# Two more column groups of a decoder layer's projections as seven quarter products

## The chip, the cores and the metric

The kernel runs on one core of a Trainium2 chip. TensorE (PE) multiplies, VectorE (DVE) and ScalarE (ACT) prepare operands and empty the accumulators, GpSimd (POOL) moves rows of tokens, and SyncE (SP) issues the loads. The metric is the device time of one execution in microseconds; lower is better.

## The reference

One decoder layer for 576 tokens (512 of a prompt, 64 of samples) with 1024 channels in float32. Cut to what the change touches:

```
z = h @ w_in                      # 1024 x 6400 columns
q, k, v, c_b, c_c, c_h, g_a, g_c = split(z)
attn = windowed attention of q, k, v
conv = c_b * short_conv(c_c * c_h)          # three taps along the tokens
merged = sigmoid(g_a) * (attn @ w_attn_out) + sigmoid(g_c) * (conv @ w_conv_out)
h = layer_norm(a * h + merged @ w_o)
h = layer_norm(a * h + experts(h) + shared(h) + ple(h))   # 64 routed experts, 6 per token
```

## The kernel before

**Groups.** The weights of the projections are loaded 256 columns at a time. Such a column group gives 2 x 128 output channels for all 576 tokens. float32 precision comes from a split of both operands into a high and a low part: a product is hi*hi + hi*lo + lo*hi. `split_hi` on ACT writes the high part of a group's weights, `split_lo` on DVE the low part (one instruction of 128x2048 each). `Step(base).v` is the number of a group; even and odd groups use one of two weight buffers each (`w_raw`, `w_hi`, `w_lo`).

**A full group** (`group`, L1225 through `chunk`) is 2 halves of channels x 8 chunks of the contraction x 3 terms x 2 halves of tokens = 96 matmuls of 288 columns, into the four banks of `proj`.

**A group in seven products** (`seven_products`, L1414 through `quarter_product`) uses Strassen's scheme in Winograd's form: weights (A) and tokens (B) are cut into 2 x 2 quarters, and 7 quarter products of 4 chunks x 3 terms = 12 matmuls each, 84 in all, give the four corners of the result. They go into the four banks of `att`, in the order a11*b11 (bank 0), s1*t1 (bank 2), s2*t2 (bank 1), s3*t3 (bank 3), a12*b21 (bank 0), s4*b22 (bank 2), a22*t4 (bank 3). A product that comes back to a bank waits until its earlier contents have been read. DVE forms the weights' sums (`s3_sum`, `s1_sum`, `s2_sum`, `s4_sum`), ACT their high parts (`s3_high`, `s12_high`, `s4_high`, `block_hi` for the plain quarters) and DVE the low ones (`block_lo`, `s3_low`, `s12_low`, `s4_low`). The sums of the tokens (t1 to t4: `t_difference`, `t_less`, `t_low`) are made once, while the attention output groups run. Results come back through `first_copy` (ACT, bank 0), `first_sums` (banks 1 and 2), `next_sums` (bank 3) and three `corner` additions (DVE).

**Order of the groups on TensorE**: attention inputs, the first two groups of the convolution, four attention output groups (`G_AO`, numbers 11 to 14), convolution groups n = 2 to 11 (numbers 15 to 24), and then four times a gate group and a convolution output group (`G_GC` = 25 and on; here GC0, CO0, GC1, CO1 ...). A triple of the convolution is n = 3m, 3m+1, 3m+2: the channels c_c, c_h and c_b. `conv_taps(m)` multiplies c_c and c_h and forms the three taps, `conv_gated(m)` multiplies by c_b and splits the result into `mix_hi` and `mix_lo`, which the CO groups read. `SEVEN` lists the n that run as seven products; the gates GC1 to GC3 do too. The order of each engine is written out by hand, an engine takes its instructions in that order, and semaphores hold them back. The waits that matter: the first product of a seven-product group waits for the low parts of its blocks (`w_ready`) and for the first corner of the seven-product group before it (`dve_read(s - 1, 3)`); the sixth waits for `first_sums` of its own group (`dve_read(s, 1)`), the seventh for `next_sums`. A CO group waits for the gate's sigmoid (`mm_free`). SP issues a load when the group two before has been split, and behind a seven-product group only when its sixth product is done, since `w_rest` lies in the raw weights.

Behind the groups come the output projection, norm, routing, shared expert and the routed experts, whose weights (192 MB) are loaded into a ring of three buffers.

## Time and profile before

| | us |
|---|---|
| median of 3 runs | 1236.82 (1236.31 to 1236.92) |
| the profiled execution | 1233.74 |
| its span, first to last instruction | 1231.9 |
| PE busy | 1195.2 (97% of the span) |
| DVE busy | 587.8 (48%) |
| ACT busy | 354.2 (29%) |
| chain that ended last | PE 50%, DMA 42%, DVE 4% |

The profile comes from one execution. Times in its rows are microseconds from the first instruction. A busy PE has matmuls in flight; since they are pipelined, the time of a group is read from its start to the next one's. Idle time in square brackets is that of the engine just before the row, with what ended it. An instruction of DVE or ACT that follows another without a wait starts some 0.1 us before that one's end, so the distance of two starts is what one costs in a row of them.

### The profile page before, as it was taken

What the parts mean: (1) busy time and instruction counts of PE and PEld (TensorE: products, weight loads), DVE (VectorE), ACT (ScalarE), POOL (GpSimd) and SP (SyncE); (2) the same over time, 40 slices, a digit from 0 to 9 for tenths busy, and PEclk for the clock granted to TensorE, in tenths of its full rate; (3) what the DMA queues carried; (4) which work ended last, traced back from release to release, by engine and by line L of the source; (5) the groups of instructions that cost most, each with busy time, mean ns of one, the idle gap of its engine ahead of it and who ended that gap; (6) DMA issues with size and microseconds to landing.
All of it is one profiled execution on the core that took longest, in us unless ns stands there. A gap on an engine that the chain in (4) does not pass through costs nothing.

```text
span 1231.9 us, 23531 instructions
## 1 busy us (share of the span) xinstructions
PE 1195.2 (97%) x8676; PEld 941.2 (76%) x8677; DVE 587.8 (48%) x1292; ACT 354.2 (29%) x704; POOL 141.5 (11%) x211
## 2 busy tenths in 40 slices
PE   8999999999999999999999999999999999999877
PEld 8999979999999999989998665555565555655543
DVE  4667774556887666677882112112212222112138
ACT  4365562333434342325022111111111111111121
POOL 0300000000000000003133121112111112121100
PEclk9999999999999999999999999999999999999999
DMA  8222123221333143624539999999999999999996
GB/s 270 75 69 69 45 64 76 42 92 44 103 103 104 38 135 93 211 82 153 229 143 367 418 420 418 421 420 421 419 420 420 420 420 418 420 422 421 422 370 282
DMA packets 98663, 307.40 MB, mean 250 GB/s; under 512 B 11244, under 2 KB 62404, under 8 KB 72840
## 3 DMA queue, kind: packets, MB, share of 16 engines
q1 hardware_dynamic: 85332, 275.20, 57.7%
q0 software_dynamic: 12304, 28.60, 6.0%
q10 hardware_dynamic: 948, 2.50, 0.6%
q8 instruction: 56, 0.92, 0.3%
q14 instruction: 23, 0.19, 0.0%
HBM read 294.45 MB, written 26.94 MB: 261 GB/s over the span
## 4 chain that ended last, share of the span: by engine, by line
PE 50%; DMA 42%; DVE 4%; issue 1%; DVEq 1%; POOL 0%; ACT 0%; SPq 0%; ACTq 0%; POOLq 0%
DMA w_exp<-in_w_e_down_dram 40%; PE proj L1225 23%; PE att L1414 8%; PE proj L1484 4%; PE proj L1635 3%; PE att L1357 1%; PE att L1319 1%; DMA fold<-expert_rows 1%; PE att L1493 1%; PE proj L1259 1%; PE proj L1579 1%; PE att L1579 1%; PE att L1370 1%; DVE res L2609 1%; PE att L1484 1%
## 5 line engine op out<-in xcount | busy, mean ns | idle before, releaser
L1709 PE MATMUL att<-w_exp,xt 128*64 128x256 f32 x2560 | 286.3, 380 | 9.1 <-DMA w_exp<-in_w_e_up_dram 7.0
L1709 PEld LDWEIGHTS att<-w_exp,xt 128*64 128x64 f32 x2560 | 191.3, 137 | 113.7 <-issue 36.2
L1729 PE MATMUL proj<-w_exp,ht_e 128*64 128x512 f32 x640 | 146.2, 598 | 3.9 <-DMA w_exp<-in_w_e_down_dram 3.9
L1225 PE MATMUL proj<-h_hi,w_hi 128*128 128x288 f32 x480 | 106.2, 303 | 0.3 <-DVE w_lo L523 0.3
L1225 PE MATMUL proj<-h_lo,w_hi 128*128 128x288 f32 x480 | 102.2, 294 | 0.0
L1225 PE MATMUL proj<-h_hi,w_lo 128*128 128x288 f32 x480 | 102.2, 295 | 0.0
L1729 PEld LDWEIGHTS proj<-w_exp,ht_e 128*64 128x64 f32 x640 | 44.2, 136 | 75.9 <-issue 71.6
L2556 DVE TENSOR_SCALAR ysb<-proj,tabw 128x512 f32 x40 | 30.0, 751 | 132.0 <-PE proj L1729 132.0
L1225 PEld LDWEIGHTS proj<-h_hi,w_hi 128*128 128x128 f32 x480 | 75.9, 189 | 6.1 <-issue 4.6
L1225 PEld LDWEIGHTS proj<-h_lo,w_hi 128*128 128x128 f32 x480 | 77.2, 188 | 0.0
L1225 PEld LDWEIGHTS proj<-h_hi,w_lo 128*128 128x128 f32 x480 | 77.0, 188 | 0.0
L2551 DVE TENSOR_TENSOR h_e<-sg,att 128x128 f32<-128x128 f32 x80 | 19.5, 286 | 116.5 <-PE att L1709 116.5
L2546 DVE TENSOR_TENSOR sg<-sg,att 128x256 f32<-128x256 f32 x40 | 16.9, 422 | 119.1 <-ACT sg L1177 119.1
L523 DVE TENSOR_TENSOR w_lo<-w_raw,w_hi 128x2048 fp32r<-128x2048 f32 x24 | 55.0, 2290 | 27.1 <-ACT w_hi L513 23.2
L1180 ACT ACTIVATE ht_e<-att 128x128 f32<-128x128 f32 x80 | 18.9, 278 | 167.9 <-PE att L1715 167.9
L1185 ACT ACTIVATE ysb<-proj,tabw 128x512 f32 x40 | 27.5, 688 | 133.2 <-PE proj L1729 133.2
L513 ACT ACTIVATE w_hi<-w_raw 128x2048 fp32r<-128x2048 f32 x24 | 45.8, 1910 | 50.5 <-PE proj L1225 37.3
L1645 PEld LDWEIGHTS proj<-ident,xg 128*128 128x128 f32 x328 | 43.6, 196 | 17.1 <-issue 12.7
L1645 PE MATMUL proj<-ident,xg 128*128 128x128 f32 x328 | 53.9, 287 | 1.5 <-DMA xg<-x_rows,gidx_col 1.5
L1225 PE MATMUL proj<-mix_hi,w_hi 128*128 128x288 f32 x256 | 54.6, 295 | 0.0
L1225 PE MATMUL proj<-mix_hi,w_lo 128*128 128x288 f32 x256 | 54.6, 295 | 0.0
L1225 PE MATMUL proj<-mix_lo,w_hi 128*128 128x288 f32 x256 | 54.5, 295 | 0.0
(475 smaller groups left out, 2292.4 us busy)
## 6 DMA issues: line engine op xcount, KB each, us to landing
w_exp<-in_w_e_gate_dram SPq DMA_DIRECT2D x64, 1024.0 KB
w_exp<-in_w_e_up_dram SPq DMA_DIRECT2D x64, 1024.0 KB
w_exp<-in_w_e_down_dram SPq DMA_DIRECT2D x64, 1024.0 KB
w_raw<-in_w_in_dram SPq DMA_DIRECT2D x21, 1024.0 KB
part<-expert_rows SPq DMA_DIRECT2D x8, 1536.0 KB, 21.3
w_raw<-in_w_in_dram SPq DMA_DIRECT2D x8, 512.0 KB
w_raw<-in_w_attn_out_dram SPq DMA_DIRECT2D x8, 512.0 KB
w_raw<-in_w_conv_out_dram SPq DMA_DIRECT2D x4, 1024.0 KB
```

The source lines that it names most:

```text
L513: nc.scalar.activation(w_hi[:, g.par, :], w_raw[:, g.par, :], ACT.Copy).then_inc(hi_done, 1)
L523: nc.vector.tensor_tensor(w_lo[:, g.par, :], w_raw[:, g.par, :], w_hi[:, g.par, :].bitcast(F32), ALU.subtract).then_inc(w_ready, 1)
L1185: nc.scalar.activation(ysb[:, bass.ds(side_of, 1), 0:512].rearrange("p o n -> p (o n)"), proj[:, 2, :], ACT.Copy, scale=tabw[:, bass.ds(k, ...
L1225: last = nc.tensor.matmul(proj[:, 2 * i + a, 0:HALF], lhs, x[:, c, a * HALF:(a + 1) * HALF], start=(c == 0 and n == 0), stop=(c == KC - 1 ...
L1414: last = nc.tensor.matmul(att[:, bank, 0:HALF], left[a][:, c, :], right[b][:, c, :], start=(c == 0 and n == 0), stop=(c == Q - 1 and n == 2))
L1484: last = nc.tensor.matmul(out, x, v, start=(c == 0 and n == 0), stop=(c == KC - 1 and n == last_term))
L1579: last = nc.tensor.matmul((proj, att)[m][:, 2 * k + a, 0:HALF], v[:, c, m * P:(m + 1) * P], x[:, c, a * HALF:(a + 1) * HALF], start=(c == ...
L1635: last = nc.tensor.matmul(gate_bank(u), x[:, c, t * P:(t + 1) * P], v[:, c, :], start=(c == 0 and n == 0), stop=(c == KC - 1 and n == 2))
L1645: last = nc.tensor.transpose(proj[:, half, c * P:(c + 1) * P], xg[:, :, half * 4 + c], ident[:, :])
L1709: last = nc.tensor.matmul(att[e * SLOT:(e + 1) * SLOT, m, 0:FF], xt[:, c, e * SLOT:(e + 1) * SLOT], weights[e][:, c, :], start=(c == 0), s ...
L1729: last = nc.tensor.matmul(proj[e * SLOT:(e + 1) * SLOT, 2 + half, :], ht_e[:, c, e * SLOT:(e + 1) * SLOT], down[e][:, c, half * 512:(half ...
L2556: nc.vector.tensor_scalar(ysb[:, bass.ds(side_of, 1), 512:D].rearrange("p o n -> p (o n)"), proj[:, 3, :], tabw[:, bass.ds(k, 1)], None, A ...
```

## The change

Two more groups run as seven quarter products: n = 2, the last group of the first convolution triple (`SEVEN` begins with 2), and the gate group GC0. Their sums and splits have places of their own in the orders of DVE and ACT, and the loads behind them wait for their sixth product.

```diff
-SEVEN = (4, 5, 7, 8, 10, 11)
+SEVEN = (2, 4, 5, 7, 8, 10, 11)
...
             for it in range(1, 4):
-                if it > 1:
-                    sp.wait_ge(st_mm, product_done(len(SEVEN) + it - 2, 5))
+                sp.wait_ge(st_mm, product_done(len(SEVEN) + it - 1, 5))
                 load(Step(G_GC + 2 * it), w_in, COL_GC + it * GW)
...
@@ ACT, while the attention output groups run
+                if k < 3:
+                    split_hi(act, Step(G_AO + k + 1))
+                else:
+                    for i in range(4):
+                        act.wait_ge(sum_raw, N_STEP + i + 1)
+                        nc.scalar.activation(t_hi[i][:, :, :], t_raw[i][:, :, :], ACT.Copy).then_inc(sum_hi, 1)
+                    block_hi(Step(G_CONV[2]))
+                    s3_high(Step(G_CONV[2]), 0)
+                    s12_high(0)
+                    s4_high(Step(G_CONV[2]), 0)
...
@@ ACT, convolution groups n = 2, 5, 8, 11
-                    first_tap(m)
+                    if m:
+                        first_tap(m)
                     first_copy(n, s)
-                    new_state(m)
-                    split_hi(act, g)
+                    if m:
+                        new_state(m)
+                    if n < 11:
+                        split_hi(act, g)
+                    else:
+                        block_hi(g)
+                        s12_high(s + 1)
+                        s4_high(g, s + 1)
+                        s3_high(g, s + 1)
+                        act.wait_ge(st_mm, product_done(s + 1, 1))
+                        act.wait_ge(u_done, 2 * m + 3)
+                        nc.scalar.activation(sig_c[:, 0, 0:HALF], att[:, 0, 0:HALF], ACT.Copy).then_inc(st_act, 1)
+                        split_hi(act, Step(G_GC + 1))
...
@@ PE
             for it in range(4):
-                if it:
-                    seven_products(Step(G_GC + 2 * it), len(SEVEN) + it - 1, moved=True)
-                else:
-                    group(Step(G_GC), h_hi, h_lo)
+                seven_products(Step(G_GC + 2 * it), len(SEVEN) + it, gate=it)
+                if it == 0:
                     pe.wait_ge(cv_lo, KC)
                 group(Step(G_GC + 2 * it + 1), mix_hi, mix_lo)
...
@@ DVE, convolution groups n = 2, 5, 8, 11
+                    if n == 2:
+                        first_sums(s)
                     next_sums(s)
-                    split_lo(dve, g)
-                    corner_11(G_CONV[n])
-                    corner_12(s)
-                    corner_21(G_CONV[n])
+                    if n < 11:
+                        split_lo(dve, g)
+                        corner_11(G_CONV[n])
+                        corner_12(s)
+                        corner_21(G_CONV[n])
+                    else:
+                        block_lo(g)
+                        s1_sum(g, s + 1)
+                        s2_sum(g, s + 1)
+                        s4_sum(g)
+                        corner_11(G_CONV[n])
+                        corner_12(s)
+                        s12_low(s + 1)
+                        corner_21(G_CONV[n])
+                        s3_sum(g, s + 1)
+                        s3_low(g, s + 1)
+                        s4_low(g, s + 1)
                     conv_gated(m)
```

For GC0 the order in which the weights' sums are made and counted is s1, s2, s4, s3 and not s3, s1, s2, s4, and `seven_products` waits for them by these counts.

**VectorE, while the attention output group number 14 runs.** Before, from the split of group 15 (n = 2) to the split of group 16:

```order
L523 TENSOR_TENSOR w_lo<-w_raw,w_hi 128x2048 [waits hi_done]
L2060 TENSOR_TENSOR gate_a<-proj,gate_a 128x576 [waits mm_ready0,sga]
L2060 TENSOR_TENSOR gate_a<-proj,gate_a 128x576 [waits mm_ready1]
L2050 TENSOR_TENSOR t_lo_98<-t_raw_102,t_hi_94 128x1152 [waits e_ready]
L2050 TENSOR_TENSOR t_lo_99<-t_raw_103,t_hi_95 128x1152 [waits e_ready]
L2050 TENSOR_TENSOR t_lo_100<-t_raw_104,t_hi_96 128x1152 [waits e_ready]
L2050 TENSOR_TENSOR t_lo_101<-t_raw_105,t_hi_97 128x1152 [waits e_ready]
L523 TENSOR_TENSOR w_lo<-w_raw,w_hi 128x2048 [waits hi_done]
```

Of the changed kernel, from the last of the t sums' low parts on:

```order
L2064 TENSOR_TENSOR t_lo_101<-t_raw_105,t_hi_97 128x1152 [waits e_ready]
L2072 TENSOR_TENSOR w_diff<-w_raw 128x4x128 [waits mm_ready1,w_dma1]
L2081 TENSOR_TENSOR s_raw<-w_raw 128x512 [waits st_out]
L2089 TENSOR_TENSOR s_raw<-s_raw,w_raw 128x512
L2102 TENSOR_TENSOR w_lo<-w_raw,w_hi 128x4x128 [waits hi_done]
L2102 TENSOR_TENSOR w_lo<-w_raw,w_hi 128x4x128 x2
L2095 TENSOR_TENSOR w_raw<-w_raw,s_raw 128x4x128
L2109 TENSOR_TENSOR w_lo<-w_diff,w_hi 128x4x128 [waits e_ready]
L2116 TENSOR_TENSOR s_lo<-s_raw,s_hi 128x512 [waits e_ready] x2
L2122 TENSOR_TENSOR w_rest<-w_raw,s_hi 128x4x128 [waits e_ready]
L2143 TENSOR_TENSOR gate_a<-proj,gate_a 128x576 [waits mm_ready0,sga]
L2143 TENSOR_TENSOR gate_a<-proj,gate_a 128x576 [waits mm_ready1]
```

The low parts of the t sums moved ahead of the last two gate products, and one split has become the preparation of a seven-product group.

**VectorE, from the next sums of n = 11 on**, that is behind the third tap of the last triple. Before (`w_lo` of the first row is GC0's, of the last CO0's; the three L2147 are the corners of n = 11):

```order
L523 TENSOR_TENSOR w_lo<-w_raw,w_hi 128x2048 [waits hi_done]
L2147 TENSOR_TENSOR prod_90<-att,prod_90 128x288 [waits mm_ready0]
L2147 TENSOR_TENSOR prod_90<-att,prod_90 128x288 [waits lg_ready]
L2147 TENSOR_TENSOR prod_91<-att,prod_91 128x288 [waits mm_ready1]
L2011 TENSOR_TENSOR prod_90<-prod_90,y_cv_88 128x512
L2012 TENSOR_TENSOR prod_90<-prod_90,y_cv_88 128x64
L2011 TENSOR_TENSOR prod_91<-prod_91,y_cv_89 128x512
L2012 TENSOR_TENSOR prod_91<-prod_91,y_cv_89 128x64
L2024 TENSOR_TENSOR mix_lo<-prod_90,mix_hi 128x576 [waits cv_hi]
L2024 TENSOR_TENSOR mix_lo<-prod_91,mix_hi 128x576 [waits cv_hi]
L523 TENSOR_TENSOR w_lo<-w_raw,w_hi 128x2048 [waits hi_done]
```

In the changed kernel the same place begins with these (the corners are L2170):

```order
L2102 TENSOR_TENSOR w_lo<-w_raw,w_hi 128x4x128 [waits hi_done]
L2102 TENSOR_TENSOR w_lo<-w_raw,w_hi 128x4x128 x2
L2081 TENSOR_TENSOR s_raw<-w_raw 128x512 [waits lg_ready]
L2089 TENSOR_TENSOR s_raw<-s_raw,w_raw 128x512 [waits lg_ready]
L2095 TENSOR_TENSOR w_raw<-w_raw,s_raw 128x4x128
L2170 TENSOR_TENSOR prod_90<-att,prod_90 128x288 [waits mm_ready0]
L2170 TENSOR_TENSOR prod_90<-att,prod_90 128x288 [waits lg_ready]
L2116 TENSOR_TENSOR s_lo<-s_raw,s_hi 128x512 [waits e_ready] x2
L2170 TENSOR_TENSOR prod_91<-att,prod_91 128x288 [waits mm_ready1]
L2072 TENSOR_TENSOR w_diff<-w_raw 128x4x128 [waits mm_ready1,w_dma1]
L2109 TENSOR_TENSOR w_lo<-w_diff,w_hi 128x4x128 [waits e_ready]
L2122 TENSOR_TENSOR w_rest<-w_raw,s_hi 128x4x128 [waits e_ready]
```

Behind them stand the four instructions of `conv_gated`, and then:

```order
L2038 TENSOR_TENSOR mix_lo<-prod_90,mix_hi 128x576 [waits cv_hi]
L2038 TENSOR_TENSOR mix_lo<-prod_91,mix_hi 128x576 [waits cv_hi]
L523 TENSOR_TENSOR w_lo<-w_raw,w_hi 128x2048 [waits hi_done]
L2156 TENSOR_TENSOR u_120<-att,sig_c 128x288 [waits lg_ready,pt_read]
L2158 TENSOR_TENSOR sig_c<-att,u_120 128x288
L2164 TENSOR_TENSOR sig_c<-att,sig_c 128x288 [waits lg_ready]
```

The one split of GC0 has become nine instructions around the corners, and the results of GC0 (from L2156 on) are read behind the split of CO0.

**ScalarE, behind the high parts of the last mix.** Before:

```order
L1036 ACTIVATE t_moved_hi<-t_hi_94 128x1152
L1036 ACTIVATE t_moved_lo<-t_lo_98 128x1152
L513 ACTIVATE w_hi<-w_raw 128x2048 [waits mm_ready1,w_dma0]
L1051 ACTIVATE sig_c<-proj 128x576 [waits mg_ready,mm_ready0]
L1051 ACTIVATE sig_c<-proj 128x576 [waits mg_ready,mm_ready1]
L1054 ACTIVATE h_hi<-t_hi_95 128x4x288
L1054 ACTIVATE h_lo<-t_lo_99 128x4x288
L950 ACTIVATE w_hi<-w_raw 128x4x128 [waits mm_ready1,w_dma1]
```

Changed:

```order
L1062 ACTIVATE sig_c<-sig_c 128x576 [waits lg_read] x2
L1065 ACTIVATE t_moved_hi<-t_hi_94 128x1152
L1065 ACTIVATE t_moved_lo<-t_lo_98 128x1152
L1067 ACTIVATE h_hi<-t_hi_95 128x4x288
L1067 ACTIVATE h_lo<-t_lo_99 128x4x288
L942 ACTIVATE w_hi<-w_raw 128x4x128 [waits mm_ready1,w_dma1]
```

All four copies of t1 and t2 now stand behind GC0's second sigmoid and before the blocks of GC1.

## Rows read from the trace of the kernel before

**Rows 1.** The chain of waits in order of time: start, us, what.
```profile
217.45 84.20 PE proj L1225 x630
...
371.73 22.25 PE att L1414 x168
393.98 25.58 PE proj L1225 x192
419.57 11.13 PE att L1414 x84
...
667.38 10.65 DMA w_exp<-in_w_e_down_dram
```

**Rows 2.** Two stretches: us, busy us of PE, PEld, DVE, ACT, POOL, clock, DMA.
```profile
393.98:406.77 12.79, 12.79 (x99) 12.79 (x98) 5.88 (x9) 5.83 (x6) 0.00 (x0) 1.00 0.66 215
490.70:667.00 176.30, 174.12 (x1317) 165.62 (x1317) 123.25 (x307) 49.30 (x73) 36.33 (x32) 1.00 0.50 183
```

**Rows 3.** Time line of DVE during attention output group 14: start, us, instruction.
```profile
263.96 1.35 DVE L2033 TENSOR_TENSOR t_raw<-h_hi 128x1152 f32<-128x1152 f32 x1
...
269.54 1.36 DVE L2043 TENSOR_TENSOR t_raw<-t_raw,h_lo 128x1152 f32<-128x1152 f32 x1
...
276.76 5.16 DVE L2050 TENSOR_TENSOR t_lo<-t_raw,t_hi 128x1152 fp32r<-128x1152 f32 x4
```

**Rows 4.** Time line of DVE, the preparation of n=4.
```profile
291.25 0.69 DVE L2076 TENSOR_TENSOR w_diff<-w_raw 128x512 f32<-128x512 f32 x1
291.85 0.69 DVE L2085 TENSOR_TENSOR s_raw<-w_raw 128x512 f32<-128x512 f32 x1
292.63 0.69 DVE L2093 TENSOR_TENSOR s_raw<-s_raw,w_raw 128x512 f32<-128x512 f32 x1
293.24 1.89 DVE L2106 TENSOR_TENSOR w_lo<-w_raw,w_hi 128x512 fp32r<-128x512 f32 x3
295.23 0.69 DVE L2099 TENSOR_TENSOR w_raw<-w_raw,s_raw 128x512 f32<-128x512 f32 x1
...
296.44 1.29 DVE L2120 TENSOR_TENSOR s_lo<-s_raw,s_hi 128x512 fp32r<-128x512 f32 x2
297.65 0.68 DVE L2126 TENSOR_TENSOR w_rest<-w_raw,s_hi 128x512 fp32r<-128x512 f32 x1
```

**Rows 5.** Time lines of SP and ACT: GC2's load is issued and first read.
```profile
429.13 0.39 SPq L549 DMA_DIRECT2D w_raw<-in_w_in_dram  x1
...
434.81 0.63 ACT L950 ACTIVATE w_hi<-w_raw 128x512 fp32r<-128x512 f32 x1 [2.90 <-DMA w_raw<-in_w_in_dram]
```

**Rows 6.** Time line of DVE at the end of n=11.
```profile
387.73 0.46 DVE L2133 TENSOR_TENSOR u<-att,prod 128x288 f32<-128x288 f32 x1 [0.61 <-PE att L1414]
...
391.09 2.28 DVE L523 TENSOR_TENSOR w_lo<-w_raw,w_hi 128x2048 fp32r<-128x2048 f32 x1
393.29 1.19 DVE L2147 TENSOR_TENSOR prod<-att,prod 128x288 f32<-128x288 f32 x3
394.57 0.69 DVE L2011 TENSOR_TENSOR prod<-prod,y_cv 128x512 f32<-128x512 f32 x1
...
396.46 1.43 DVE L2024 TENSOR_TENSOR mix_lo<-prod,mix_hi 128x576 fp32r<-128x576 f32 x2
```

**Rows 7.** Time line of ACT: a copy of t2, and GC1's second sigmoid.
```profile
408.41 1.16 ACT L1054 ACTIVATE h_lo<-t_lo 128x1152 fp32r<-128x1152 f32 x1
...
431.23 0.69 ACT L1047 ACTIVATE sig_c<-sig_c 128x576 f32<-128x576 f32 x1 [0.91 <-DVE sig_c L2147]
```

**Rows 8.** Time line of DVE: the second product of CO0's results.
```profile
419.68 0.76 DVE L2235 TENSOR_TENSOR prod<-proj,sig_c 128x576 f32<-128x576 f32 x1 [1.90 <-PE proj L1225]
```

**Rows 9.** Time line of PE at the start; waits of PE, 217 to 667 us.
```profile
1.07 5.38 PE L1238 MATMUL att<-warm 128*128 128x128 f32 x26 [1.07 <-POOL warm L740]
...
11.28 1.73 PE L1266 MATMUL proj<-warm 128*128 128x128 f32 x14
...
PE proj L1608 <- DVE tab_b L2475: 2.1, 2, 1.2
```

More of the change, by code:

```diff
@@ L973, in s4_high @@
                 nc.scalar.activation(s4_hi[:, :, :], quarter(w_raw, g, 1, 0), ACT.Copy).then_inc(sum_hi, 1)
+            for k in range(4):
+                nc.scalar.activation(gate_a[:, 2 * k:2 * k + 2, :], gate_a[:, 2 * k:2 * k + 2, :], ACT.Sigmoid).then_inc(sga, 1)
+                if k < 3:
[8 more added lines that the diff above has]
+                    s4_high(Step(G_CONV[2]), 0)
             def first_tap(m):
@@ L1416, in quarter_product, with seven_products @@
                 return last
-            def seven_products(g, s, moved=False):
+            def seven_products(g, s, gate=None):
                 a11, a12, s3, a22 = (tuple(quarter(w, g, k, n) for w in (w_hi, w_lo))
@@ L1425, in seven_products @@
                 t1, t2, t3, t4 = (tuple(v[k][:, :, :] for v in (t_hi, t_lo)) for k in range(4))
-                if moved:
+                if gate:
                     t1 = tuple(v[:, :, :] for v in t1_moved)
@@ L1429, in seven_products @@
                 s4 = (s4_hi[:, :, :], quarter(w_rest, g, 1, 0))
-                for i in range(0 if moved else 2):
+                for i in range(2 if gate is None else 0):
                     nc.tensor.sem_inc(mm_free[i], 1)
@@ L2110, in s3_low @@
             def s3_low(g, s):
[L2112 removed]
+                dve.wait_ge(sum_hi, sum_count(s, 4 if s == len(SEVEN) else 1))
                 nc.vector.tensor_tensor(quarter(w_lo, g, 0, 1), quarter(w_diff, g, 0, 1),
```

102 lines of the change are left out of this document (51 added, 51 removed).

## The prediction, written before the changed kernel ran

> **What bounds the kernel now.** I read the chain of waits first: from 217.45 us on it is TensorE alone, group after group without a gap (84.20 us of full groups, then 22.25 us for two seven-product groups, 25.58 us for two full ones, 11.13 us for one), up to the routing, and from 667.38 us on it is the loads of the expert weights [rows 1]. The table of stretches says the same: TensorE is busy for all 12.79 us of the first gate group at granted clock 1.00, and for 174.12 of the 176.30 us from there to the experts [rows 2]. The expert loads are issued when work on TensorE and VectorE is done, so what moves the end of the last gate group moves the end of the program by as much. Nothing behind it has a start of its own. The stretch to look at is therefore 217 to 491 us, and the question is only whether TensorE stays without gaps. The time lines of VectorE and ScalarE answer it.
>
> **What the change removes from TensorE.** A full group is 96 matmuls, a group in seven products 84. They cost 25.58 / 2 = 12.79 us and 11.13 us [rows 1], so each converted group saves 1.66 us, and two save 3.32 us if no product waits.
>
> **Group n=2 (the last of the first triple).** Its weights must now be prepared by VectorE while the last attention-output group runs (263.31 to 276.1 us). The last five instructions of the raw t sums (263.96 to 270.90, 6.9 us) come one group, 12.8 us, earlier and end at about 258; ScalarE has the four high parts at about 259.4. The four low parts (5.16 us, at 276.76 before) now stand where the raw sums stood, at 263.96 [rows 3], and end at about 269.1. The preparation of a seven-product group is the row of nine instructions that n=4 has at 291.25 to 298.33, 7.1 us [rows 4]. Put at 269.05 it gives the low parts of the blocks (all that the first product needs) at about 273.0, s1 and s2 by 275.5, s4 by 276.1. TensorE wants the first at 276.1 and s1 at 277.7. VectorE's two gate products of that group follow, at 276.05 and 276.7; nobody writes their banks before 287. The next group's load now waits for n=2's s4 product (285.6) and by the 5.7 us that such a load takes [rows 5] it lands at 291.3, and VectorE gets to it at about 291.1 anyway; its preparation ends at 298.5, its blocks at 295.2, against a start at 300.0. So n=2 has cover everywhere: **-1.66 us**.
>
> **The first gate group (GC0).** Here three seven-product groups follow each other (n=10, n=11, GC0), and VectorE's order is what counts. I use the profile's clock as if n=2 had not been made shorter. VectorE waits for TensorE for the last time at 387.73; from there it is busy without a break. At 391.09 it stood before the 2.20 us split of the full group, followed at 393.29 by the three corners (0.37 us apart) that free the att banks [rows 6]. Now it has, from 391.09: three block parts 1.81, s1 0.79, s2 0.78, s4 0.61 [rows 4]. The first corner starts at 395.08 and is done at 395.53. GC0's first product writes bank 0, which that corner reads, so it waits for it; n=11 ends at 393.98. That is a gap of 395.57 - 393.98 = **1.6 us**. Before, GC0 was a full group and wrote proj, so the corners did not hold it.
>
> From there on VectorE runs: two corners 0.74, s1 and s2 low 1.21, third corner 0.37, the s3 difference 0.69, ScalarE's high part of it 0.66 (which nothing fills), s3 low 0.60, s4 low 0.78 with the drain. The gated product begins at 400.2 instead of 394.57. It and the two low parts of mix take until 403.4 (394.57 to 397.81 before), the split of CO0's weights 2.20 more, to 405.6 [rows 6]. Only then comes the first sum of GC0 (two instructions of 0.46 us with a drain between them, 1.0 us): done at 406.6. TensorE has started GC0 at 395.57 and wants to begin its sixth product, which overwrites bank 2, after five of 1.59 us, at 403.5. The sixth waits for that first sum, so a second gap: 406.64 - 403.52 = **3.1 us**. The fifth to seventh product see no other wait: ScalarE's copy of bank 0 is done at about 399.1, the next sums by 407.5 against the seventh product at 408.2. GC0 ends at 409.8, where it ended at 406.77: 11.13 + 1.6 + 3.1 = 15.8 us against 12.79, **+3.0 us**. Put together: between the fourth product of n=11 and the sixth of GC0 VectorE has 16 us of work where TensorE has 12.7 (eight products of 1.59).
>
> Both bounds of this term: if ScalarE's 0.66 and all drains (0.1 each, four of them) could be hidden, it would be about 1.1 less; if CO0's load, which is issued at 392.4, lands as late as ScalarE could have noticed before (399.1), or the hand-overs cost 0.1 instead of 0.04, some 0.5 more. I take the middle, since the rows of n=4 and n=11 repeat to within 0.02 us.
>
> **The second gate (GC1) and later.** CO0 now starts at E = 409.8. GC1's load, which was issued at 393.40 before, waits for GC0's s4 product and lands near E + 4.1, as GC2's did (wait until 434.81 with the end of GC1 at 430.70) [rows 5]. ScalarE, though, first has the second sigmoid (it starts 0.53 after E, as at 431.23) and now all four copies of t1 and t2 (1.06 us each), two of which stood before the first gate until now. It gets to GC1's blocks at E + 5.4, and VectorE ends the preparation at E + 12.0 [rows 4, 7]. The two products of CO0's results come behind it, the second at E + 13.5 instead of E + 12.9 (419.68 against 406.77) [rows 8]. The chain to GC1's first sum then ends 8.1 us after GC1's start, not 7.5, and the sixth product wants it at 7.95: a gap of about **0.2 us**. GC2 and GC3 keep the pattern that they have.
>
> **The sum.** -1.66 + 3.0 + 0.2 = +1.6 us. The profiled execution took 1233.74 us, 1231.9 of it its span; it would become 1235.3 and 1233.5. The median of the runs shown, 3.1 us higher, goes from 1236.82 to **1238.4 us**.
>
> A row and a page differ over the size of the saving. Twelve fewer matmuls are 12 x 0.133 = 1.6 us by the rows [rows 1]. The Trainium skill (TensorE: Matmul & The Clock Gate, Back-to-back issue gap) puts the gap between isolated matmuls at N / 2.4 + 2.5 ns, 122.5 ns for 288 columns; as an estimate from that page, 24 matmuls save 2.94 instead of 3.32 us and the sum would be some 0.4 us higher. I stay with the rows.
>
> **The rivals.** (1) *VectorE keeps up* and both gaps are absent: the whole 3.32 us comes out, 1233.5 us. It needs the 16 us between 389 and 406 to shrink to 12.7. For it speaks that the same instructions for n=10 leave no gap; against it, that n=10 has no gated product, no mix and no full split between its preparation and the next first sum. In between lies a case in which one of the gaps is half of what I count: 1235.5 to 1237. (2) *The gap costs the clock*, the slower side: the only waits of TensorE that the view of waits lists between 217 and 667 us are two of 2.1 us together, at granted clock 1.00 [rows 2, 9], and now it stands for 3.1 us in one piece. If the matmuls behind it run as the first ones of the program did (26 fillers in 5.38 us, where 14 later ones took 1.73, 0.124 each), the loss is 5.38 - 26 x 0.124 = 2.2 us once [rows 9]: 1240.6 us. It decides from the point where GC0's second gap is long enough. Against it: the profile gives granted clock 1.00 even for those first 5.38 us, and its only lower stretch lies behind the last matmul of the program.
> The Trainium skill (the same page, Why this matters for your kernels) says that a long enough idle between bursts of matmuls sends the array back to half rate. That is this rival; no row of this trace shows it in mid-program.
> (3) *A load becomes late*: n=4's and GC1's loads are the two that are held back. Each has over 1 us of cover (ScalarE is busy until E + 5.4, n=4's blocks are ready 4.8 us early), so it would cost under 1 us and stays inside the forecast's range. That the change leaves the kernel's order as it was is excluded: the rows of the two orders differ as shown.
>
> **How the numbers follow.** The forecast (1237.4 to 1239.4) gets 0.65, the case between 0.08, VectorE keeping up 0.10, the clock 0.17. A measurement of this kernel can tell some 0.2%, 2.5 us, from no change. Faster than 1234.3: rival 1 and a little of the case between, 0.12. Slower than 1239.3: rival 2 and 0.05 of the forecast's upper end, 0.22. Within: 0.66. The range that leaves out rival 1 and the upper half of rival 2 is 1235.2 to 1240.8.
>
> **What would show it.** In the changed trace: an att group of 84 matmuls in 11.1 us where n=2 is; two TensorE gaps in GC0, about 1.6 us before its first product behind a corner on VectorE and about 3.1 us before its sixth behind the first sum; CO0's start 1.4 us later than 406.77 on the trace's clock (-1.66 + 3.05); a gap of 0.2 us or none in GC1. I am wrong if TensorE has no gap in GC0, if the corners start before 394, if n=2 or n=4 waits for its weights, or if the stretch behind 491 us changes in length.

## The result and the profile after

| | before | changed |
|---|---|---|
| median, us | 1235.99 (1233.79 to 1238.57, 20 runs) | 1238.01 (1235.76 to 1239.78, 20 runs) |
| ratio of the times, 95% interval | 1 | 1.0020 (1.0014 to 1.0026) |
| profiled execution and its span, us | 1233.74, 1231.9 | 1239.67, 1237.7 |
| n=2 to the end of CO3, us | 214.70 | 219.05 |

The change costs 0.2%, about 2.5 us (1.7 to 3.2). A second set of runs of the changed kernel gave 1.0027 (1.0017 to 1.0038). It is slower than before, by little. The last line of the table is the stretch in which all of the change lies. The chain of waits of the changed kernel (start, duration, what; x counts matmuls) shows where it became longer:

```profile
277.55 11.13 PE att L1427 x84
...
371.54 19.45 PE att L1427 x147
390.99 1.80 DVE w_lo L2102 x3
...
406.53 4.96 PE att L1427 x24
...
432.52 3.41 PE att L1427 x24
```

Before, this chain was TensorE without a break [rows 1]. n=2 is now a group of 84 matmuls in 11.13 us. But the chain leaves TensorE at 390.99 and comes back only at 406.53, for the last two products of GC0. Those 24 matmuls take 4.96 us where the same two products of GC1 take 3.41 (the last row). The time line of TensorE has three rows with idle time between 394 and 434 us:

```profile
395.48 0.37 PE L1427 MATMUL att<-h_hi,w_hi 128*128 128x288 f32 x1 [1.69 <-DVE prod L2170]
406.53 0.37 PE L1427 MATMUL att<-h_hi,s_hi 128*128 128x288 f32 x1 [2.86 <-DVE sig_c L2158]
432.52 0.37 PE L1427 MATMUL att<-h_hi,s_hi 128*128 128x288 f32 x1 [0.32 <-DVE sig_c L2158]
```

The first is GC0's first product, behind the first corner of n=11; the second is its sixth, behind the first sum; the third is GC1's sixth. VectorE's time line says what it did meanwhile, and answers [rows 6]:

```profile
390.91 1.89 DVE L2102 TENSOR_TENSOR w_lo<-w_raw,w_hi 128x512 fp32r<-128x512 f32 x3
...
394.88 0.81 DVE L2170 TENSOR_TENSOR prod<-att,prod 128x288 f32<-128x288 f32 x2
...
398.57 0.69 DVE L2109 TENSOR_TENSOR w_lo<-w_diff,w_hi 128x512 fp32r<-128x512 f32 x1 [0.70 <-ACT w_hi L949]
...
399.95 0.69 DVE L2025 TENSOR_TENSOR prod<-prod,y_cv 128x512 f32<-128x512 f32 x1
...
403.19 2.28 DVE L523 TENSOR_TENSOR w_lo<-w_raw,w_hi 128x2048 fp32r<-128x2048 f32 x1
405.39 0.45 DVE L2156 TENSOR_TENSOR u<-att,sig_c 128x288 f32<-128x288 f32 x1
405.92 0.46 DVE L2158 TENSOR_TENSOR sig_c<-att,u 128x288 f32<-128x288 f32 x1
```

The corner starts at 394.88, the gated product at 399.95, the split for CO0 at 403.19, and only then the first sum, done at 406.4. The 0.70 us in brackets is ScalarE's high part of s3. What the prediction did not have in its sum stands in the table of stretches (the columns are busy shares of PE, PEld, DVE, ACT and POOL, then the granted clock, the share of the DMA engines and GB/s):

```profile
403.70:406.50 2.80, 0.00 (x0) 0.00 (x1) 2.62 (x4) 0.00 (x0) 0.00 (x0) 1.00 0.00 0
406.50:407.00 0.50, 0.47 (x4) 0.50 (x4) 0.50 (x2) 0.00 (x0) 0.00 (x0) 1.00 0.00 0
407.00:408.00 1.00, 1.00 (x9) 1.00 (x8) 0.67 (x2) 0.00 (x0) 0.00 (x0) 0.77 0.00 0
408.00:409.00 1.00, 1.00 (x6) 1.00 (x6) 0.05 (x1) 0.00 (x0) 0.00 (x0) 0.50 0.00 0
409.00:410.00 1.00, 1.00 (x6) 1.00 (x6) 0.41 (x1) 0.56 (x1) 0.00 (x0) 0.50 0.01 3
410.00:411.00 1.00, 1.00 (x6) 1.00 (x6) 0.00 (x0) 0.12 (x1) 0.00 (x0) 0.53 0.67 90
411.00:412.00 1.00, 1.00 (x10) 1.00 (x9) 0.46 (x1) 0.00 (x1) 0.00 (x0) 1.00 1.03 354
```

TensorE stood still for 2.86 us, started again at 406.53, and from about 407.5 to 411 the granted clock was 0.50 (1.2 GHz, the lower of its two levels). TensorE is full in these rows. The number behind x counts every matmul that is in flight at some time in the row, so it says less than the starts do: in the time line the matmuls start 0.24 us apart at clock 0.50, four in a microsecond, and 0.133 us apart, seven or eight, at 1.00. That costs 4.96 - 3.41 = 1.6 us.

### The profile page after: what moved, and what is told of

The parts are those of the page before. It is cut to its first block, busy times and chain, and to the rows that moved or that the text cites. A ratio compares the mean times of both kernels' runs of the same rounds, so it can differ in the third digit from the quotient of the medians.

```text
span 1237.7 us, 23555 instructions
## 1 busy us (share of the span) xinstructions
PE 1197.6 (97%) x8652; PEld 941.1 (76%) x8653; DVE 602.9 (49%) x1324; ACT 359.1 (29%) x718; POOL 140.8 (11%) x211
## 4 chain that ended last, share of the span: by engine, by line
PE 49%; DMA 41%; DVE 6%; issue 1%; DVEq 1%; ACT 1%; SPq 0%; ACTq 0%; POOLq 0%
DMA w_exp<-in_w_e_down_dram 39%; PE proj L1238 20%; PE att L1427 9%; PE proj L1498 4%; PE proj L1649 3%; PE att L1370 1%; PE att L1332 1%; PE att L1507 1%; PE proj L1272 1%; PE proj L1593 1%; DMA fold<-expert_rows 1%; PE att L1593 1%; PE att L1383 1%; PE att L1676 1%; DVE res L2646 1%
## 5 line engine op out<-in xcount | busy, mean ns | idle before, releaser
L1238 PE MATMUL proj<-h_hi,w_hi 128*128 128x288 f32 x416 | 92.5, 304 | 0.3 <-DVE w_lo L523 0.3
L1238 PE MATMUL proj<-h_lo,w_hi 128*128 128x288 f32 x416 | 88.9, 295 | 0.0
L1238 PE MATMUL proj<-h_hi,w_lo 128*128 128x288 f32 x416 | 88.8, 295 | 0.0
L1238 PEld LDWEIGHTS proj<-h_hi,w_hi 128*128 128x128 f32 x416 | 65.6, 188 | 6.1 <-issue 4.6
L1238 PEld LDWEIGHTS proj<-h_lo,w_hi 128*128 128x128 f32 x416 | 67.0, 189 | 0.0
L1238 PEld LDWEIGHTS proj<-h_hi,w_lo 128*128 128x128 f32 x416 | 66.9, 189 | 0.0
L523 DVE TENSOR_TENSOR w_lo<-w_raw,w_hi 128x2048 fp32r<-128x2048 f32 x22 | 50.4, 2289 | 26.4 <-ACT w_hi L513 20.7
L810 POOL DMA_INDIRECT expert_rows<-ysb,sidx_col x39 | 39.5, 1012 | 124.8 <-DVE ysb L2593 124.8
```

The costliest lines, as they stand in the source:

```text
L523: nc.vector.tensor_tensor(w_lo[:, g.par, :], w_raw[:, g.par, :], w_hi[:, g.par, :].bitcast(F32), ALU.subtract).then_inc(w_ready, 1)
L810: pool.indirect_dma_start(out=rows_d[:, :], out_offset=bass.IndirectOffsetOnAxis(ap=sidx_col[i][:, 0:1], axis=0), in_=ysb[:, i, :], in_off ...
L1238: last = nc.tensor.matmul(proj[:, 2 * i + a, 0:HALF], lhs, x[:, c, a * HALF:(a + 1) * HALF], start=(c == 0 and n == 0), stop=(c == KC - 1 ...
```

## The experiments

I compare the kernels in two ways: by the ratio of times to runs of the kernel before on the same chip, and by the length of the stretch from the start of n=2 to the end of CO3 in the one profiled execution of each, which leaves out what happens elsewhere. One correction belongs to the stretch: a CO group takes 12.80 or 12.49 us, and the same kernel has either, so I count every CO group as 12.80 (+0.31 us for each short one).

| kernel | stretch, us | CO groups at 12.49 | as if all 12.80 | to before | ratio of the times (95%) |
|---|---|---|---|---|---|
| before | 214.70 | 2 | 215.32 | | 1 |
| changed | 219.05 | 0 | 219.05 | +3.7 | 1.0020 (1.0014 to 1.0026) |
| after_again | 219.03 | 0 | 219.03 | +3.7 | 1.0027 (1.0017 to 1.0038) |
| n2_only | 213.02 | 2 | 213.64 | -1.7 | 0.9989 (0.9978 to 1.0000) |
| n2_again | 213.60 | 0 | 213.60 | -1.7 | 0.9997 (0.9988 to 1.0006) |
| gc0_only | 220.22 | 1 | 220.53 | +5.2 | 1.0048 (1.0033 to 1.0063) |
| dve_more | 222.30 | 0 | 222.30 | +7.0 | 1.0049 (1.0035 to 1.0063) |
| fill | 217.44 | 0 | 217.44 | +2.1 | 1.0020 (1.0008 to 1.0031) |
| fill_again | 217.43 | 0 | 217.43 | +2.1 | 1.0021 (1.0010 to 1.0032) |
| sums_first | 215.84 | 1 | 216.15 | +0.8 | 0.9999 (0.9989 to 1.0009) |
| late_mix | 216.64 | 1 | 216.95 | +1.6 | 1.0006 (0.9997 to 1.0015) |
| keep_up | 215.83 | 0 | 215.83 | +0.5 | 0.9996 (0.9987 to 1.0005) |
| early_copies | 212.26 | 3 | 213.19 | -2.1 | 0.9977 (0.9968 to 0.9986) |

My theory: n=2 has cover and saves its 1.66 us; all of the loss is at GC0, where VectorE has more to do before GC0's first sum than TensorE gives it time for, because work for CO0 stands ahead of it, and the stop that this makes draws the half clock. The rivals: the loss comes from n=2 having let TensorE run ahead; VectorE's total work decides, whatever its order; the half clock has nothing to do with the stop.

**Each half of the change alone.**

n2_only is the changed kernel with its second half undone:

```diff
-                seven_products(Step(G_GC + 2 * it), len(SEVEN) + it, gate=it)
+                if it:
+                    seven_products(Step(G_GC + 2 * it), len(SEVEN) + it - 1, gate=it)
+                else:
+                    group(Step(G_GC), h_hi, h_lo)
```

gc0_only has its first half undone:

```diff
-SEVEN = (2, 4, 5, 7, 8, 10, 11)
+SEVEN = (4, 5, 7, 8, 10, 11)
```

The orders of VectorE, ScalarE and SyncE go with them in both kernels.

> Only group n=2 runs as seven products; the first gate group (GC0) is a full group of 96 matmuls again, with the orders of VectorE and ScalarE that the kernel before has there. My theory (the two conversions add up, n=2 is worth -1.66 us and GC0 costs all the rest): no gap of TensorE between 217 and 490 us, GC0 in 12.8 us, the time 1.7 us below the kernel before. Rival (the loads or the preparation behind n=2 have moved and cost something further on, so that n=2 has no gain of its own): the same time as the kernel before, with 11.13 us for n=2 in the trace and the gain lost between there and the end of the gates.

> Only GC0 runs as seven products; n=2 is a full group again and its preparation stands where the kernel before has it. By the trace of the changed kernel GC0 takes 17.7 us instead of 12.8: my theory (the two gaps and the half clock behind them belong to GC0 alone) expects gaps of 1.7 and 2.9 us before its first and sixth product, about 3.4 us at half clock behind them, and a time 4.0 to 5.5 us above the kernel before. If the half clock was an accident of the one execution that was profiled: 3.2 to 3.6 us above. Rival (the gaps come from n=2, which lets TensorE run ahead of VectorE by 1.66 us more): the gaps shrink to 0 and 2 us, and the time is within 1 us of the kernel before.

The chain of n2_only has TensorE alone again, two full groups in one piece behind n=10 and n=11:

```profile
369.72 22.26 PE att L1423 x168
391.98 25.58 PE proj L1234 x192
```

Its stretch is 1.68 us shorter than before with the same number of short CO groups, against 1.66 expected. The times say -0.11% and, in a second set (expected: 0.9987), -0.03%; both intervals reach -0.12%, and the first touches no change. The saving is as large as predicted in the trace; in the times it is about half of that and at the edge of what can be measured.

> The kernel with only n=2 converted, once more, beside the one with all copies moved early, to tell which of the two is the faster. Expected from its trace: 1.6 us below the kernel before (ratio 0.9987), every group from n=2 to CO3 without a gap.

gc0_only has the same gaps as the changed kernel, 1.68 and 2.86 us, and is 0.48% slower than before, 5.9 us where 4.0 to 5.5 were expected. The rival (n=2 makes the gaps by letting TensorE run ahead) is excluded: without n=2 the gaps are as long. In the stretch the two halves add up: -1.70 + 5.21 = +3.5, and the changed kernel has +3.7. Its rows of stretches show more on the clock:

```profile
406.00:407.00 1.00, 0.00 (x0) 0.00 (x0) 1.00 (x2) 0.00 (x0) 0.00 (x0) 1.00 0.00 0
407.00:408.00 1.00, 0.00 (x0) 0.00 (x0) 0.83 (x3) 0.00 (x0) 0.00 (x0) 0.74 0.00 0
408.00:409.00 1.00, 0.94 (x4) 0.97 (x5) 0.99 (x3) 0.00 (x0) 0.00 (x0) 0.50 0.00 0
```

Here the clock falls while TensorE is still standing (PE busy 0.00 in the row with 0.74); in the changed kernel it fell when TensorE had been running again for about 1 us. So it isn't the restart that draws it.

**The half clock.** Two kernels test whether it belongs to the stop: one with the stop filled, one with a longer stop.

fill, in `seven_products` ahead of the sixth product:

```diff
                 pe.wait_ge(sum_ready, lo_count(s, 4))
+                if gate == 0:
+                    for _ in range(20):
+                        nc.tensor.matmul(proj[:, 0, 0:HALF], h_hi[:, 0, 0:P], h_hi[:, 0, 0:HALF], start=True, stop=True)
                 pe.wait_ge(st_dve, dve_read(s, 1))
```

dve_more, on VectorE in the loop over the gates:

```diff
+                if it == 0:
+                    dve.wait_ge(hi_done, G_GC + 2)
+                    nc.vector.tensor_tensor(w_lo[:, 0, :], w_raw[:, 0, :], w_hi[:, 0, :].bitcast(F32), ALU.subtract)
+                    dve.drain()
                 split_lo(dve, Step(G_GC + 2 * it + 1))
```

> The changed kernel with 20 extra matmuls of 288 columns (2.7 us at 0.133 each) between the fifth and the sixth product of GC0, where TensorE waits for VectorE's first sum. They write a bank that nothing reads before it is overwritten, and the results do not change. Theory A (the stop of 2.9 us is what halves the clock for the 3.4 us behind it): granted clock 1.00 through the whole of GC0, the sixth and seventh product in 3.2 us, the time 1.8 us below the changed kernel. Theory B (the lower clock comes from the whole pattern of the last 15 us, or is an accident of one execution): the time equals the changed kernel's, and the stretch at half clock is still there, or was not usual in it.

> The changed kernel with the split of CO0's weights done twice on VectorE (2.3 us more with its drain, the same values written), ahead of GC0's first sum. Theory (VectorE is what the sixth product waits for, one to one): the second gap grows from 2.9 to 5.1 us and CO0 starts 2.3 us later: 2.3 us above the changed kernel. The clock: if a longer stop of TensorE draws the half clock more surely, there is a stretch at half clock behind it in the trace, and the time is up to 1.8 us more than that, 2.3 to 4.1 us above. If the half clock has nothing to do with the stop, the time is 2.3 us above and the profiled execution has such a stretch in this place no more often than elsewhere.

> The changed kernel itself once more, beside the others on the same chip. The trace shows whether the half clock behind GC0's second gap, and the one at 175 us long before the change, are there in every execution. If they belong to the gap: again a stretch at half clock within 2 us of the end of the gap. If they are drawn anew in each execution: one of the two or both are missing, and the span is shorter by 1.7 us for each one missing ahead of 660 us. The time: 2 to 3 us above the kernel before.

> The kernel with 20 extra matmuls in GC0's second gap once more. Its trace showed no half clock behind the gap and 1.6 us less between n=2 and the end of CO3 than the changed kernel, while the medians of the two stood at the same ratio to the kernel before. If the half clock belongs to the gap: again none at 407 us, and the time 0.5 to 2 us below the changed kernel, whose two ratios were 1.0020 and 1.0027. If the gain of the trace is given back elsewhere: the ratio is again 1.002 or more.

The stretches at the end of the stop, of after_again, of fill_again and of dve_more:

```profile
407.00:408.00 1.00, 1.00 (x7) 1.00 (x6) 0.19 (x1) 0.00 (x0) 0.00 (x0) 0.55 0.00 0
408.00:409.00 1.00, 1.00 (x6) 1.00 (x6) 0.46 (x1) 0.08 (x1) 0.00 (x0) 0.50 0.00 0
```

```profile
408.00:409.00 1.00, 1.00 (x10) 1.00 (x9) 0.24 (x1) 0.69 (x1) 0.00 (x0) 1.00 0.20 29
```

```profile
407.00:408.00 1.00, 0.00 (x0) 0.00 (x0) 1.00 (x2) 0.00 (x0) 0.00 (x0) 0.61 0.00 0
408.00:409.00 1.00, 0.29 (x1) 0.32 (x2) 0.83 (x3) 0.00 (x0) 0.00 (x0) 0.50 0.00 0
...
413.00:414.00 1.00, 1.00 (x6) 1.00 (x6) 0.00 (x0) 0.14 (x1) 0.00 (x0) 0.50 0.57 115
414.00:415.00 1.00, 1.00 (x9) 1.00 (x8) 0.43 (x1) 0.00 (x0) 0.00 (x0) 0.97 0.97 327
```

after_again shows both answers to its question: the stretch at 175 us is missing and the one behind GC0's gap is there. All four profiled executions in which GC0 has a stop of 2.85 us or more (the changed kernel twice, gc0_only, dve_more) have the half clock there; both with the stop filled have 1.00 all through GC0, and their stretch is 1.6 us shorter for it. With a stop of 5.2 us, in one execution, the lower level lasts twice as long, about 6.8 us. dve_more's stretch is 3.25 us longer than the changed kernel's: 2.37 for the longer stop, which is one to one what was added on VectorE (2.3), and 0.9 because the last two products took 5.84 us instead of 4.96. By the ratios it is 2.7 to 3.6 us above the changed kernel (3.1 by the medians on the chip where both ran), inside the expectation with the clock. The half clock belongs to the stop, then, and theory A holds in the trace. The rule of the Trainium skill that the prediction named (TensorE: Matmul & The Clock Gate, Why this matters for your kernels) says that idle between bursts sends the array back to half rate. These four traces agree; but it speaks of longer stops than those of 1.65 to 2.6 us elsewhere in the program, behind which the clock fell in some of the executions here (below), and there the measurement decides.

The times don't confirm the 1.6 us. fill stands at 1.0020 and 1.0021, the changed kernel at 1.0020 and 1.0027: a difference of -0.1 to 0.9 us with an uncertainty of more than 1, between runs that did not stand side by side. From the end of CO3 to the end of the program, the two executions with the filled stop took 742.0 us each and the two of the changed kernel 741.1 and 740.6. The granted clock of that part says where this can come from. Both filled executions have three stretches of 3.4 us at 0.50 there (at 803, 1165 and 1192 us), the changed kernel has one (at 807) and after_again none, behind stops that the other kernels have there or close by. One such place, of after_again and of fill, each behind a stop of 2.6 us:

```profile
805.00:806.00 1.00, 1.00 (x12) 0.83 (x10) 0.00 (x0) 0.00 (x0) 0.00 (x0) 1.00 1.01 418
```

```profile
804.00:805.00 1.00, 1.00 (x8) 0.66 (x6) 0.00 (x0) 0.00 (x0) 0.00 (x0) 0.50 1.01 422
```

Over all 13 traces this part takes 741.6 to 743.1 us in the five with two or three such stretches, and 740.3 to 741.5 us in the eight with one or none. So the clock further on can give back as much as the filled stop gained. Whether filling the stop brings these stretches about or they fell there by chance is not shown (late_mix, which isn't filled, has the same three). What the half clock behind GC0's stop costs in the time is therefore between 0 and 1.6 us.

**The order on VectorE.**

sums_first moves the split for CO0, on VectorE in the loop over the gates:

```diff
-                split_lo(dve, Step(G_GC + 2 * it + 1))
+                if it:
+                    split_lo(dve, Step(G_GC + 2 * it + 1))
                 first_sums(s, raw_gate)
                 next_sums(s, raw_gate)
                 corner_11(G_GC + 2 * it, raw_gate)
+                if it == 0:
+                    split_lo(dve, Step(G_GC + 1))
```

> The changed kernel with one instruction moved on VectorE: the split of CO0's weights (2.2 us) stands behind GC0's first sums, next sums and first corner, no longer ahead of them. Theory (the sixth product waits for what VectorE is made to do first, so the order decides): first sum ready at 404.3 instead of 406.5, the gap before the sixth product 0.7 us instead of 2.9, no stretch at half clock; then CO0 waits for the split, the second corner and the sigmoid, about 2 us, and starts 2.8 us earlier than in the changed kernel: 1235.2 us. If the half clock is not usual in the changed kernel: 1.0 us below it. Rival (VectorE's total work up to CO0 decides, whatever its order): the gap only moves from the sixth product to the start of CO0, which starts where it did, and only the half clock, if it goes, changes the time.

One instruction in another place takes 0.21% off the changed kernel's 0.20%: the time is that of the kernel before. The list of waits of TensorE (waiting group, what it waited for: us in total, times, longest):

```profile
PE att L1427 <- DVE prod L2170: 1.7, 1, 1.7
PE proj L1238 <- ACT sig_c L1062: 1.2, 1, 1.2
PE att L1427 <- DVE sig_c L2158: 0.7, 1, 0.7
```

The gap before the sixth product is 0.7 us as expected, there is no stretch at half clock, and a new wait of 1.2 us stands before CO0, for the sigmoid. The sum of the gaps fell from 4.6 to 3.6 us and the half clock's 1.6 went with it: CO0 starts 131.5 us behind n=2 instead of 133.9, 2.4 us earlier where 2.8 were expected. Order decides more than the total does, but the wait at CO0 shows that the total was still too much. The next kernel takes away from that place what CO0 alone needs.

In late_mix TensorE's wait for mix moves from ahead of CO0 into `chunk`:

```diff
+                if c == KC - 2 and i == 0 and g.base == G_GC + 1 and g.v == G_GC + 1:
+                    pe.wait_ge(cv_lo, KC)
```

VectorE's `conv_gated(3)` no longer follows `s4_low` of n=11, and in the loop over the gates:

```diff
-                split_lo(dve, Step(G_GC + 2 * it + 1))
+                if it:
+                    split_lo(dve, Step(G_GC + 2 * it + 1))
                 first_sums(s, raw_gate)
+                if it == 0:
+                    split_lo(dve, Step(G_GC + 1))
                 next_sums(s, raw_gate)
                 corner_11(G_GC + 2 * it, raw_gate)
                 corner_12(s, raw_gate)
+                if it == 0:
+                    conv_gated(3)
                 corner_21(G_GC + 2 * it, raw_gate)
```

On ScalarE GC0's first sigmoid stands ahead of the copies of mix of n=11.

> The changed kernel with VectorE relieved of what only CO0 needs: behind n=11 it skips the gated product and the low parts of mix (3.2 us) and goes on with GC0's first sums, then the split of CO0's weights, next sums, the first two corners, and only then the gated product; ScalarE does GC0's first sigmoid ahead of mix; TensorE waits for mix before the last two chunks of CO0's first half instead of before CO0. Theory (the sixth product waits only because 5.4 us of work for CO0 stand ahead of GC0's first sum): no gap before the sixth product, the gap of 1.7 us before the first product stays, CO0 starts 11.1 us behind GC0's start, 2.2 us earlier than with the sums first: 3.0% of 1.66 in words, as the full group did, 1.6 to 2.0 us below the kernel before. Rival (the total of VectorE's work decides): the waits come back as a stop in the middle of CO0 and behind it, and the time stays at that of the kernel before.

(The sum meant there is 1.6 to 2.0 us below the kernel before.) The first part came true: only the gap of 1.7 us at GC0's start is left, and CO0 starts 11.2 us after GC0. Yet the time is 0.06% above the kernel before and not 0.15% below:

```profile
PE att L1432 <- DVE prod L2173: 1.7, 1, 1.7
PE att L1432 <- ACT sig_c L1062: 1.4, 1, 1.4
PE att L1432 <- DVE sig_c L2161: 1.2, 1, 1.2
```

The second and the third are in GC1, before its fifth and its sixth product. The rival had said that waits would come back behind CO0, and they did, though not where it had put them and not through VectorE's total. keep_up has them as well.

keep_up is late_mix with another order on VectorE at n=11:

```diff
+                        corner_11(G_CONV[n])
                         block_lo(g)
                         s1_sum(g, s + 1)
                         s2_sum(g, s + 1)
-                        s4_sum(g)
-                        corner_11(G_CONV[n])
                         corner_12(s)
-                        s12_low(s + 1)
-                        corner_21(G_CONV[n])
+                        s12_low(s + 1, (0,))
                         s3_sum(g, s + 1)
+                        s4_sum(g)
+                        s12_low(s + 1, (1,))
                         s3_low(g, s + 1)
-                        s4_low(g, s + 1)
+                        corner_21(G_CONV[n])
```

In the loop over the gates `s4_low` of GC0 follows `first_sums`, and the split for CO0 follows `next_sums`.

> As the kernel with the late mix, and VectorE's preparation of GC0 is put in order of need: the first corner of n=11 ahead of the blocks, then blocks, s1, s2, second corner, low part of s1, s3, s4, low part of s2 and of s3, third corner, first sums, low part of s4, next sums, the split for CO0. Theory (each product waits for one step on VectorE, and the work fits if it comes in order of need): no gap above 0.3 us in front of any product of GC0, GC0 in 11.1 to 11.8 us, and the whole saving of both groups, 3.32 us less 0.3 to 0.6: 2.6 to 3.2 us below the kernel before. Rival (VectorE has not time enough): the gap of 1.7 us only moves from the first product to the second to fourth, and the time equals that of the kernel with the late mix.

GC0's first gap is gone, and the waits are these:

```profile
PE att L1432 <- DVE sig_c L2163: 1.2, 1, 1.2
PE att L1432 <- ACT sig_c L1062: 1.1, 1, 1.1
PE att L1432 <- DVE s_lo L2121: 0.2, 1, 0.2
```

GC0 has one listed wait of 0.2 us and takes 12.2 us up to CO0, a little more than the 11.1 to 11.8 expected. VectorE had time enough for GC0. The expectation that 2.6 to 3.2 us would come out failed on GC1, which takes 13.9 us instead of 11.1. ScalarE's time line shows why:

```profile
408.77 0.69 ACT L1065 ACTIVATE sig_c<-sig_c 128x576 f32<-128x576 f32 x1 [1.20 <-DVE sig_c L2175]
409.36 1.15 ACT L1068 ACTIVATE t_moved_hi<-t_hi 128x1152 fp32r<-128x1152 f32 x1
...
413.58 0.62 ACT L942 ACTIVATE w_hi<-w_raw 128x512 fp32r<-128x512 f32 x1
```

The second sigmoid starts 2.9 us after CO0 has started (405.8) because the gated product now stands before the third corner, then come four copies, and GC1's blocks wait behind them. The last kernel spreads the copies.

On top of keep_up, early_copies takes the four copies out of the loop over the gates on ScalarE and puts them in three places:

```diff
                         block_hi(g)
+                        for old, new in ((t_hi, h_hi), (t_lo, h_lo)):
+                            nc.scalar.activation(t2_moved(new), old[1][:, :, :].bitcast(F32), ACT.Copy)
                         s12_high(s + 1)
...
                         split_hi(act, Step(G_GC + 1))
+                        nc.scalar.activation(t1_moved[0][:, :, :], t_hi[0][:, :, :].bitcast(F32), ACT.Copy)
...
+            nc.scalar.activation(t1_moved[1][:, :, :], t_lo[0][:, :, :].bitcast(F32), ACT.Copy)
             for it in range(4):
```

> As the kernel whose VectorE keeps up, and the four copies of t1 and t2 on ScalarE (1.06 us each), which stand behind GC0's second sigmoid, are spread: both of t2 behind the blocks of GC0 while ScalarE is idle, the first of t1 behind the split for CO0, the second behind the copies of mix. Theory (the 2.9 us that GC1 loses in the kernel that keeps up come from ScalarE, which gets to GC1's blocks only at 413.6, behind these copies, so that the preparation, CO0's products, the split for CO1 and the copy of bank 0 all stand late): GC1 in 11.1 to 11.6 us instead of 13.9, the stretch from n=2 to the end of CO3 2.3 to 2.8 us shorter, and the time 1.7 to 2.6 us below the kernel before. Rival (what holds GC1 is its load or VectorE): GC1 still takes over 13 us and the time stays where it was, 0.0 to 0.8 us below the kernel before.

```profile
PE att L1431 <- DVE s_lo L2120: 0.2, 1, 0.2
```

That is the whole list of waits of TensorE from 200 to 510 us. The chain:

```profile
369.88 19.81 PE att L1431 x150
...
404.17 13.02 PE proj L1242 x96
417.19 11.13 PE att L1431 x84
```

and ScalarE gets to GC1's blocks 3.8 us after CO0's start instead of 7.8:

```profile
407.12 0.69 ACT L1069 ACTIVATE sig_c<-sig_c 128x576 f32<-128x576 f32 x1
407.92 0.63 ACT L942 ACTIVATE w_hi<-w_raw 128x512 fp32r<-128x512 f32 x1
```

GC1 takes 11.13 us. The time is 0.23% below the kernel before (0.14 to 0.32%), 2.8 us, a little more than the 1.7 to 2.6 expected. This kernel beats the changed one and the one before.

It doesn't bring the whole 3.32 us, though, and most of what it brings is n=2. GC0 takes 12.2 us from its start to CO0's, as in keep_up, where a group in seven products without waits takes 11.13: the second and the third product and CO0 each start 0.2 to 0.35 us late, of which the list shows only the first. In the stretch early_copies is 0.4 us shorter than n2_only and n2_again (213.19 against 213.64 and 213.60). The times say more: 0.9977 against 0.9989 and, on the same chip, 0.9997, which is 1.5 and 2.5 us. Only the second pair of intervals is apart. Converting GC0 too was worth making with another order around it, by 0.4 us in the trace and perhaps more in the time.

## Why the prediction was right, and where it was not

The forecast was 1238.4 us and the median is 1238.01. That is closer than the reasoning deserves. The forecast was a loss of 1.6 us on a starting point of 1236.82; with 20 runs the starting point is 1235.99 and the loss 2.5 us, in the second set 3.3. The sign and the place were right, the size was 0.9 to 1.7 us too small. Point by point:

- **n=2, -1.66 us**: right. The traces of the kernels with n=2 alone give -1.68 and -1.72 in the stretch, no wait stands at n=2 or n=4.
- **GC0's first gap, 1.6 us behind the first corner of n=11**: right, 1.69. Putting the corner first removed it (keep_up).
- **GC0's second gap, 3.1 us behind the first sum**: right, 2.86. Its reading, that the sixth product waits one to one for what VectorE does before it, is shown by dve_more: 2.3 us more there, 2.37 more of a gap.
- **GC1, 0.2 us**: too small. GC1 took 11.67 us, 0.5 more than 11.13: the time line lists 0.32 as a wait at the sixth product, which starts 0.48 us late. The chain was the one described: sigmoid, four copies, blocks (at 416.81, 5.3 us after CO0's start, 5.4 predicted), preparation, CO0's products, first sum.
- **Rival 1** (VectorE keeps up) fell as the change stands, and came true in the main once the order was changed: both long gaps went, but of its 3.32 us the best kernel has 2.1 in the stretch. Its argument against itself, that VectorE has 16 us of work where TensorE has 12.7, took the order as given: 3.2 us of that were the gated product and the low parts of mix, and 2.2 us the split for CO0, which GC0 doesn't need. I had the bound right for this order and did not ask what in it could wait.
- **Rival 3** (a late load) didn't occur.

By the stretch, the terms as measured are -1.66 + 4.91 (GC0 at 17.70 instead of 12.79) + 0.53 (GC1) = +3.8 us; the table has +3.7. The times give 2.5 and 3.3. The rest of 0.4 to 1.2 us is not explained; one profiled execution each, with its own course of the clock and of the CO groups' pace, is too few to follow it.

## What to carry to other kernels

Count what the slower partner must do before the sum that a product waits for, and then ask of each step in that row who needs it: here 5.4 us of work for the next group stood ahead of a sum for the current one, and moving one 2.2 us instruction was worth as much as the change had lost. When a stop of the array can't be avoided, keep it short, because the matmuls behind it may pay again; filling it took the half clock away from there in both traces, but no run shows that the time got shorter by it. Don't take a clock of 1.00 in the first microseconds of a profile as a measurement: look at how far apart the matmuls start. And when one engine is relieved by moving work, look at the group after the next: late_mix gained 2.2 us over sums_first up to CO0 and lost 3.1 at GC1, through copies on ScalarE that had looked free.

## What the runs showed of the hardware that I had not expected

- **The clock takes another course in every execution, also of the same kernel.** At 172.2 to 175.2 us, long before the change, TensorE stops for 1.65 us in every kernel here. In 5 of 13 traces a stretch at half clock follows (in the changed kernel as below), in 8 none does, that of the kernel before among them:

```profile
173.00:174.00 1.00, 0.00 (x0) 0.00 (x0) 0.83 (x6) 0.19 (x1) 0.00 (x0) 1.00 0.00 0
174.00:175.00 1.00, 0.90 (x11) 0.84 (x12) 0.85 (x6) 1.00 (x6) 0.00 (x0) 1.00 0.00 0
175.00:176.00 1.00, 1.00 (x8) 1.00 (x7) 1.00 (x5) 0.47 (x1) 0.00 (x0) 0.71 0.00 0
176.00:177.00 1.00, 1.00 (x6) 0.99 (x5) 0.80 (x6) 0.34 (x1) 0.00 (x0) 0.50 0.00 0
```

  It moves n=2's start from 276.05 to 277.55 us (1.5 us of the 5.8 by which the profiled spans of before and after differ). Over 29 runs of the kernel before, the mean granted clock of an execution lies between 0.992 and 0.999 and the time goes with it: 1233.7 us on average for the six at 0.998, 1237.4 for the two at 0.993. In two later sets of 24 runs the time goes the same way, less clearly (0.5 and 0.4 us for each 0.001 of the clock, where these 29 give 0.8). A part of the spread of this kernel's times goes with the clock, then.
- **The pace of the CO groups.** The same 96 matmuls take 12.49 or 12.80 us (0.130 or 0.133 each) at granted clock 1.00, in the same kernel from one execution to the next: n2_only has two short ones, n2_again none. I don't know what decides it.
- **A longer stop, a longer half clock**: 3.4 us behind 2.86 us of idle (three traces), about 6.8 behind 5.2 (one).
